# A chunkwise RWKV-7, retention and mixture-of-experts layer: the 64x64 inverses of the chunks computed ahead, in the projection

## The reference

```python
def step(S, inp):
    r_t, w_t, k_t, v_t, kk_t, b_t = inp
    S = (S * w_t[:, :, None, :]
         + jnp.einsum('bhvk,bhk->bhv', S, -kk_t)[..., None] * b_t[:, :, None, :]
         + v_t[..., None] * k_t[:, :, None, :])
    return S, jnp.einsum('bhvk,bhk->bhv', S, r_t)
```

## Time and profile before

| | us |
|---|---|
| median of 3 runs | 1478.66 |
| lowest and highest run | 1476.57, 1480.93 |
| profiled execution, span | 1474.4 |
| TensorE busy in it | 1409.7 (96%) |
| VectorE busy | 1035.8 (70%) |
| ScalarE, GpSimd busy | 708.2, 566.9 |

### The profile page before, as it was taken

The page is one execution under the profiler, slowest core; times in us unless marked ns, Lnnn a source line. Parts: engine busy times, 40 slices in busy tenths (PEclk is TensorE's granted clock), DMA queues, the critical chain, the costliest instruction groups (busy, mean ns, idle before and its releaser), DMA issues. The chain is left out here.

```text
span 1474.4 us, 30049 instructions
## 1 busy us (share of the span) xinstructions
PE 1409.7 (96%) x12906; PEld 1229.6 (83%) x12906; DVE 1035.8 (70%) x1190; ACT 708.2 (48%) x694; POOL 566.9 (38%) x203
## 2 busy tenths in 40 slices
PE   5999999999999899999999879999999999999994
PEld 5999999999997788888888658888888888888881
DVE  6456655544214867877777668999899898777766
ACT  5533542212223322222222247777777777777763
POOL 1001101000000300000000148777878878999985
PEclk9999999999999999999999989999999999999997
DMA  6145565643328443434332499999999999999968
GB/s 217 44 144 182 164 187 173 203 133 124 97 81 290 120 113 113 144 96 145 110 101 74 145 380 406 404 404 415 412 415 404 412 402 408 413 416 414 416 262 350
DMA packets 125358, 366.08 MB, mean 248 GB/s; under 512 B 11680, under 2 KB 79264, under 8 KB 113200
## 3 DMA queue, kind: packets, MB, share of 16 engines
q1 hardware_dynamic: 113296, 321.48, 59.1%
q0 software_dynamic: 6912, 25.17, 4.7%
q10 hardware_dynamic: 5040, 17.83, 3.0%
HBM read 295.47 MB, written 68.98 MB: 247 GB/s over the span
## 5 line engine op out<-in xcount | busy, mean ns | idle before, releaser
L1131 PE MATMUL ps<-u_hi,w_hi 128*128 128x352 f32 (+1 forms) x720 | 236.9, 329 | 4.9 <-DVE u_lo L781 4.9
L1131 PE MATMUL ps<-u_lo,w_hi 128*128 128x352 f32 (+1 forms) x720 | 232.7, 323 | 0.0
L1131 PE MATMUL ps<-u_hi,w_lo 128*128 128x352 f32 (+1 forms) x720 | 231.8, 322 | 0.0
L2783 POOL TENSOR_TENSOR down_lo<-down_raw,down_hi 128x1024 fp32r<-128x1024 f32 x31 | 150.9, 4869 | 61.4 <-ACT down_hi L2846 61.4
L2939 DVE TENSOR_TENSOR down_lo<-down_raw,down_hi 128x3072 fp32r<-128x3072 f32 x31 | 124.0, 4000 | 42.4 <-ACT down_hi L2846 42.4
L1131 PEld LDWEIGHTS ps<-u_hi,w_hi 128*128 128x128 f32 x720 | 136.7, 190 | 11.9 <-issue 5.8
L1131 PEld LDWEIGHTS ps<-u_hi,w_lo 128*128 128x128 f32 x720 | 136.5, 190 | 0.0
L1131 PEld LDWEIGHTS ps<-u_lo,w_hi 128*128 128x128 f32 x720 | 136.5, 190 | 0.0
L1550 POOL TENSOR_TENSOR mix_stat<-mix_stat,minus_half 128x4 f32<-128x4 f32 x8 | 8.4, 1055 | 317.2 <-DVE mix_stat L1921 317.2
L2846 ACT ACTIVATE down_hi<-down_raw 128x4096 fp32r<-128x4096 f32 x31 | 112.7, 3636 | 19.6 <-ACT y_out L2867 19.6
L3162 PE MATMUL ps<-first_up_hi,x_hi 128*128 128x512 f32 x256 | 104.1, 407 | 4.7 <-DVE up_lo L2939 3.3
(11 more groups left out here) (489 smaller groups left out, 3511.5 us busy)
## 6 DMA issues: line engine op xcount, KB each, us to landing
down_raw<-in_moe_w_down SPq DMA_DIRECT2D x32, 2048.0 KB, 11.0
second_gate_raw<-in_moe_w_gate SPq DMA_DIRECT2D x16, 2048.0 KB, 10.5
second_up_raw<-in_moe_w_up SPq DMA_DIRECT2D x16, 2048.0 KB, 9.9
gate_raw<-in_moe_w_gate SPq DMA_DIRECT2D x15, 2048.0 KB, 10.6
up_raw<-in_moe_w_up SPq DMA_DIRECT2D x15, 2048.0 KB, 9.6
tm_rows<-tm_stage SPq DMA_DIRECT2D x32, 512.0 KB, 3.2
y_slots<-y_out ACTq DMA_DIRECT2D x31, 512.0 KB, 11.5
w_raw<-in_w_in SPq DMA_DIRECT2D x30, 512.0 KB, 4.2
```

Source lines behind the costliest of these rows:

```text
L1131: mm = pe.matmul(z_of(n, r_), w[n % 3][:, k_, :], a[:, k_, c0:c1], start=(k_ == 0 and i == 0), stop=(k_ == KD - 1 and i == 2))
L2783: pool.tensor_tensor(lo[e % 2][:, cut:, :], raw[e % 2][:, cut:, :], hi[:, cut:, :].bitcast(F32), ALU.subtract).then_inc(sem(f"{name}_lo2_r ...
```

## The change

The inverses of all 128 triangles (8 heads, 16 chunks) are computed once, in `project`, and `mix` loads them.

- TensorE's new `grams(q)` multiplies the decayed `b_d` with `a_d`, 32 matmuls of 64x64 for each `q`, into the two turning banks; it stands ahead of the turn of `a`, which moves behind the LoRA products. VectorE masks them to `gram`, and SyncE stores them (`gram_blocks`).
- Ahead of block 15 SyncE loads all of them as `triangles`: one triangle on each of 128 partitions, 64x64 in its 4096 elements.
- VectorE solves by forward substitution, `solve(steps)`: for row `i` one product of column and row over `i` x (63 - `i`) elements into `terms` (printed as `ln_rows`), and one addition, which waits for it. The 62 steps are spread over blocks 16 to 29 by the budgets `SOLVE_US`, each group behind `low(n + 2)`. By them the groups have 4, 7, 2, 5, 0, 4, 1, 4, 3, 4, 4, 5, 5 and 14 steps. The last writes ones on the diagonal (`solved`).
- SyncE stores the inverses with eight DMAs, one for each head, from 16 partitions each, in runs of 64 floats, and waits for them ahead of the barrier.
- The copies of the second halves of `rg` and `rv` move from VectorE to ScalarE.
- In `mix`, `load_inv(t)` brings 256 KB for each tile. All products and additions that made the inverse go, with their copies on ScalarE; `solved(t)` multiplies the loaded inverse with (`a` | `q_m`), and ScalarE copies the result to `w_m`. The product of `a` and `b` goes too. The body is written in another order on TensorE, VectorE and ScalarE, and body 1 has an order of its own.

```diff
-            order += [(name, q - 1, f) for name in ("a", "bh", "kh", "v", "gate") for f in range(2)]
+            order += [(name, q - 1, f) for name in ("g", "a", "bh", "kh", "v", "gate") for f in range(2)]
...
+SOLVE_FROM = NB - 14
+SOLVE_US = (3.0, 9.5, 3.0, 9.0, 1.0, 9.0, 1.0, 9.0, 9.0, 9.0, 9.0, 10.0, 11.0)
...
+def solve_steps():
+    cost = lambda i: 2 * (i * (C - 1 - i) / 956 + 0.16)
+    ends, i, spare = [], 1, 0.0
+    for budget in SOLVE_US:
+        spare += budget
+        while i < C - 1 and cost(i) <= spare:
+            spare -= cost(i)
+            i += 1
+        ends.append(i)
+    ends.append(C - 1)
+    return [range(a, b) for a, b in zip([1] + ends[:-1], ends)]
...
+        tri = nc.alloc_sbuf_tensor_at("triangles", [P, C, C], F32, offset=solve_at)
...
+        terms = ln_rows[:].rearrange("p i c -> p (i c)")
+        gram = cum[:, 0:2 * NTX * C].rearrange("p (n c) -> p n c", c=C)
...
+                        sp.wait_ge(sem("gram_ready"), 2 * (q + 1))
+                        for c in range(2):
+                            sp.dma_start(gram_dram[q, :, c].rearrange("n s t -> s n t"), gram[c * C:(c + 1) * C]
+                                         ).then_inc(sem("gram_stored"), 16)
...
+                        sp.dma_start(tri[:], gram_dram.rearrange("q n c s t -> (q n c) s t")).then_inc(sem("gram_loaded"), 16)
...
+                sp.wait_ge(sem("solved"), 1)
+                for h in range(HA):
+                    sp.dma_start(inv_dram[:, h * C:(h + 1) * C].rearrange("(n s) t -> n s t", s=C), tri[h * 2 * NTX:(h + 1) * 2 * NTX]
+                                 ).then_inc(sem("inv_stored"), 16)
...
+                sp.wait_ge(sem("inv_stored"), 16 * HA)
...
+                def grams(q):
+                    for f in range(2):
+                        i = FILL["g", q, f]
+                        dve.wait_ge(sem("filled"), i + 1)
+                        dve.tensor_tensor(gram[:, f * NTX:(f + 1) * NTX, :], ps[:, 5 + i % 2, :].rearrange("p (n c) -> p n c", c=C),
+                                          cst("lt").unsqueeze(1).to_broadcast([P, NTX, C]), ALU.mult).then_inc(sem("gram_ready"), 1)
+                def solve(steps):
+                    for i in steps:
+                        w = C - 1 - i
+                        term = terms[:, 0:i * w].rearrange("p (m n) -> p m n", n=w)
+                        if i == 1:
+                            dve.wait_ge(sem("gram_loaded"), 16)
+                        else:
+                            dve.wait_ge(sem("solve_step"), i - 1)
+                        dve.tensor_tensor(term, tri[:, 0:i, i:i + 1].to_broadcast([P, i, w]), tri[:, i:i + 1, i + 1:C].to_broadcast([P, i, w]),
+                                          ALU.mult).then_inc(sem("solve_term"), 1)
+                        dve.wait_ge(sem("solve_term"), i)
+                        dve.tensor_tensor(tri[:, 0:i, i + 1:C], tri[:, 0:i, i + 1:C], term, ALU.add).then_inc(sem("solve_step"), 1)
+                    if steps and steps[-1] == C - 2:
+                        dve.wait_ge(sem("solve_step"), C - 2)
+                        dve.memset(tri[:].rearrange("p s t -> p (s t)")[:, 0:C * C:C + 1], 1.0).then_inc(sem("solved"), 1)
...
+                                if r_ == 0:
+                                    grams(i - 1)
...
-                        if kind == "rv":
-                            if i == 0:
-                                ret_gate(3)
-                                rg_turned(3)
-                            else:
-                                turned(("rv", i - 1), tm_rv[i - 1], ("tm_kd_stored", 32))
+                        if kind == "rv" and i == 0:
+                            ret_gate(3)
...
+                        if n >= SOLVE_FROM:
+                            solve(SOLVE[n - SOLVE_FROM])
...
+                def grams(q):
+                    pe.wait_ge(sem("a_d_ready"), 2 * (q + 1))
+                    pe.wait_ge(sem("b_d_ready"), q + 1)
+                    banks = [bank_of(("g", q, a)) for a in range(2)]
+                    for t in range(NTX):
+                        for a, c in ((0, 0), (1, 1), (0, 1), (1, 0)):
+                            rows, cols = slice(a * C, (a + 1) * C), slice(N_META + t * P + c * C, N_META + t * P + (c + 1) * C)
+                            mm = pe.matmul(banks[a][c * C:(c + 1) * C, t * C:(t + 1) * C], b_d[rows, cols], a_d[rows, cols], start=True, stop=True)
+                    mm.then_inc(sem("filled"), 2)
...
+                            if i > 0 and r_ == 0:
+                                grams(i - 1)
+                            if i > 0 and r_ > 0:
                                 after_k(i - 1, r_)
                             lora_ups(i, r_)
+                            if i > 0 and r_ == 0:
+                                after_k(i - 1, r_)
...
+                def load_inv(t):
+                    sp.dma_start(inverse[:, t % 2, :], inv_dram[(t - 1) * P:t * P, :]).then_inc(sem(f"inv_loaded{t % 2}"), 16)
...
+                load_inv(2)
+                load_heads(2)
                 load_retention(2)
-                load_heads(2)
...
+                def w_copy(t):
+                    copy(w_m[:].rearrange("p h j c -> p (h j c)"), ps[:, 0:2, :].rearrange("p a c -> p (a c)"), "w_done", t, "w_m_ready")
...
                 def body(t):
+                    a_mean(n)
                     masked(ak_t, one_of(2, 0), "lt", "g_k_done", t, "ak_t_ready")
                     masked(rk_t[:], one_of(2, 1), "le", "g_k_done", t, "rk_t_ready")
+                    masked(rb_t, bank_pair(4), "le", "g_b_done", t, "rb_t_ready")
+                    a_centre(n)
+                    if n >= 2:
+                        logits_of(n - 1)
+                    a_variance(n)
+                    if n >= 2:
+                        choose_group(n - 1)
+                    a_gate(n)
+                    b_centre(t)
+                    if n >= 2:
+                        choose_first(n - 1)
+                    if t + 1 < NT:
+                        memories(t + 1)
+                    b_gate(t)
                     if t + 1 < NT:
                         scores(t + 1)
+                    keep(t, 0)
+                    rz_rows(t)
+                    low_a(n)
+                    state_first(t)
+                    low_b(t, 3)
+                    keep(t, 1)
+                    if n >= 2:
+                        choose_second(n - 1)
+                    residual(n, 0)
+                    residual(n, 1)
+                    h_variance(n)
+                    state_last(t)
+                    y_rows(t)
+                    norm(n)
...
+                def solved(t):
+                    chunks_by_two(0, inverse[:, t % 2, :], two_rows(TM_NAMES.index("a"), QM_ROW)).then_inc(sem("w_done"), 1)
...
+                def body(t):
+                    n = t - 1
+                    features_loaded(t)
+                    pe.wait_ge(sem("y_ready"), n)
+                    pe.wait_ge(sem("s_t_ready"), t)
+                    keys_of(t)
+                    pe.wait_ge(sem("state0_ready"), n)
+                    pe.wait_ge(sem("crossed"), t)
+                    removals_of(t)
+                    if n >= 3:
+                        pe.wait_ge(sem("ranks_read"), n - 2)
+                    if n >= 2:
+                        route_sum(n - 1)
+                    ret_rows_1(n)
+                    pulled(t)
+                    ret_rows_0(n)
+                    pe.wait_ge(sem("y0_ready"), n)
+                    pe.wait_ge(sem("in_s_ready"), t)
+                    solved(t)
+                    pe.wait_ge(sem("rk_t_ready"), t)
+                    if t + 1 < NT:
+                        ret_keys(t + 1)
+                        ret_scores(t + 1)
+                    steps_of(t)
+                    turn_y(n)
+                    if t + 1 < NT:
+                        pe.wait_ge(sem("memory_ready"), t + 1)
+                    added(t)
+                    pe.wait_ge(sem("m_t_ready"), t)
+                    pe.wait_ge(sem("n_m_done"), t)
+                    advance(4, m_t[:, 0, :], state[0]).then_inc(sem("s1_done"), 1)
+                    if t + 1 < NT:
+                        pe.wait_ge(sem("s_t_ready"), t + 1)
+                    turn_ret(t, 3)
+                    rwkv_rows_0(n)
+                    pe.wait_ge(sem("state1_ready"), t)
+                    advance(5, m_t[:, 1, :], state[1])
+                    pe.wait_ge(sem("rz_t_ready"), t)
+                    if t + 1 < NT:
+                        ret_inner(t + 1)
+                    rwkv_rows_1(n)
+                    own_rows(t)
+                    pe.wait_ge(sem("b_lo_ready"), t)
+                    state_rows(t)
+                    turn_h2(n)
+                    if t + 1 < NT:
+                        ret_cross(t + 1)
+                    pe.wait_ge(sem("h2_t0_ready"), n)
+                    if n >= 3:
+                        rows_of(n - 2)
+                    if n >= 2:
```

(2 more changed lines are left out.)

501 lines of the change are left out of this document (192 added, 309 removed).

## The result

The changed kernel takes 1459.55 us (median of 4 runs, 1457.76 to 1460.66), the kernel before 1477.62 us; the ratio is 0.987, with an interval of 0.985 to 0.989. That is 18 us less, where 44 were forecast; the time lies in the upper part of the stated range of 1404 to 1464. The profiled execution has a span of 1455.8 us, 25.7 more than the sum of the prediction gave.

A forecast was written before the change was run, and what follows sets the result against it. TensorE was taken to bound the projection and mixing. Span: 1474.4 + 50.8 (mixing begins later) - 97.1 (shorter mixing) + 2.0 (clock) = 1430.1 us, so 1434 for the median of runs; range 1404 to 1464.

The forecast's parts named there:

- Mixing bodies: Mixing loop, bodies 2 to 8: 33.5 us for a middle body instead of 46.4; 232.2 us in sum, 86.1 less.
- the walk: Mixing body: VectorE's and TensorE's queues in the new order, priced from the end of `state_rows`; the body ends at 33.5 us.
- Gram products: Projection, TensorE: four times 32 matmuls at 0.95 us plus about 0.8 us more each, 7.1 us.
- Price of the substitution: Projection, VectorE: 1.04 ns an element and 0.185 us for each dependent operation, 109.7 us for all 62 steps.
- Stops of TensorE: Projection: TensorE stops 7.0 and 6.0 us for rotated keys (blocks 20, 22), 3.7 us for gates (blocks 24, 26).
- The store: Between solve and mixing: 2048 KB in runs of 256 B from 16 partitions take 20 us, bounds 8 and 40.
- Body 2: Second body of the mixing: 34.5 us, with GpSimd splitting `w_out` beside it.
- Body 1: First body of the mixing: 43 us instead of 54.1, 11 less, waiting for loads such as `load_heads(2)`.
- Behind body 8: Last rows, routing and experts, behind 817 us: only the order of the first few instructions changes.
- The clock as a term: Begin of the mixing: TensorE's clock falls after the longer stop at the barrier; 2 us added, 0 to 6.
- Rival B: Projection's stops and store are short: solve ends at 460, store takes 8 us, kernel 1407 or less; chance 0.13.

## Why the prediction was right or wrong

- **Mixing bodies: right.** The products, masks and additions taken out gave what their rows said; bodies 3 to 8 came out 1.9 us below the walk, of 195.8.
- **Gram products: right.** 7.1 us forecast, 6.7 measured.
- **Price of the substitution: right.** 0.90 us for 686 elements; the groups behind the last split took 38.7 us, 38.0 forecast.
- **Stops of TensorE: right in place, too small.** 7.0, 6.0 and 3.7 us were forecast, 9.8, 5.8 and 3.2 measured, 2.1 more in all. The step that failed for the first one is that the split ahead of the group would come when it had come before, moved by the Gram products alone. It came some 3 us later, since ScalarE waited 3.0 us for a load of weights that SyncE issued late. What I had not priced either is the clock behind a stop: the last split moved by 30.3 us, of which the Gram products are 6.7 and the stops 18.8, and 4.8 are left. The windows of 8 us behind the two long stops have a clock of 0.78 and 0.68, which is 1.8 and 2.6 us:

```profile
338.32:346.32 8.00, 8.00 (x46) 7.89 (x47) 3.60 (x6) 0.46 (x1) 0.00 (x0) 0.78 0.47 135
370.70:378.70 8.00, 7.99 (x41) 7.89 (x42) 2.83 (x5) 2.12 (x5) 0.00 (x0) 0.68 0.45 131
```

  Together the mixing begins 8.8 us late: 2.1 of stops, 4.8 of clock, 0.7 of the last groups and 1.6 of the store, less 0.4 of the Gram products.
- **The store: right in size, for a half-right reason.** 22.1 us against 20.5. I had put it down to the 16 partitions; the runs of 256 B and their longer issue carry as much, 6.9 us, as the eight issues from 16 partitions do.
- **Body 2: mis-sized, 34.5 against 41.0.** The prediction saw GpSimd's splits beside VectorE and gave them 1 us. They doubled the time of VectorE's own splits, and `b_rows(2)`, which frees TensorE's bank, stood behind these. The run that moves GpSimd's work brought the body to 34.6, the 34.5 of the forecast.
- **Body 1: mis-sized, 43 against 48.0.** About 3.2 us are the time of one load behind 2 MB of `w_out` and the next inverse on the same queue, which I had named and taken too short. The other 1.8 are open. The clock at its begin is not the cause; the clock within the body, 0.73, may be: in the run with eleven fillers behind body 8, whose edit leaves body 1 alone, it took 46.1 us at 0.79.
- **Behind body 8: wrong, and the largest term, 9.4 us.** The failing step is the sentence that of the instructions behind 817 us only the order of the first few changes. The body was walked from one `state_rows` to the next, and so the turn of `h2` and the routing, which had stood ahead of the mark, were dropped for the last tile. That is 4 to 5 us; 3 to 4 are clock that this execution lost. 1.4 lie within the experts, which take 617.2 to 620.6 us in the 16 profiled executions, 618.8 before and 620.2 in the changed kernel: no effect of the change can be read from them.
- **The clock as a term: 2 us, too small,** and in the wrong place. I had put it at the begin of the mixing; what the runs show is 4.8 us behind the stops in the projection and 3 to 4 behind body 8.
- **Rival B was the right question.** It gave 1407 or less, if the stops and the store were short. Nothing in the changed kernel is so, but the same work in another order gives 1423.8, and with the other store, body 2's two edits, larger budgets and the earlier issue of the store 1400.5.

## What to carry to other kernels

Work that fills an engine's idle time must stand in its queue ahead of the instruction that would wait, not behind it: the same 110 us cost some 30 to 36 us on one side of the split of weights and nothing measurable on the other. A late instruction also delays what stands behind its results in another queue, here a load of weights behind a store. Where a marker instruction is used to measure a loop, list what has moved from one side of it to the other, or the last round's share is lost. A full engine that is stopped for long pays for the stop and then for the clock: here 9.8 and 5.8 us of stops, and 4.3 us behind them. Behind the two stops of under 2 us the clock stayed at 1.00.
